# The value projection of both mixers multiplied unsplit in fp32, in a three-block network on one core

## The reference, cut to what matters

```python
for l in range(2):
    h = rms_norm(x, norm1_g[l]) * (1.0 + scale1) + shift1
    z = h @ w_in[l]                       # [256,1024] @ [1024,4608]
    q, k = z[..., 0:512], z[..., 512:1024]            # rotated, 4 heads x 2 x 64
    v    = z[..., 1024:1536]                          # 4 heads x 128
    o = diff_attention(q, k, v, lam)                  # two softmaxes, one minus lam times the other
    y_attn = rms_norm(o, subln_g[l]) * c @ w_attn_o[l]
    u = ga * sigmoid(gb); u = silu(layer_norm(conv31(u)))
    y_conv = u @ w_conv_o[l]
    x = x + (1 + gate1) * ((g_attn * y_attn + g_conv * y_conv) @ w_out[l])
    x = x + (1 + gate2) * ((silu(f_gate) * f_up) @ w_ffn_out[l])
```

## Time and profile before

| | us |
|---|---|
| median of 3 runs (2473.72 to 2474.51) | 2473.92 |
| the profiled execution, its own time | 2476.07 |
| span of the profile | 2474.3 |

### The profile page before, as it was taken

How to read it: one execution, slowest core, us unless ns; L and a number is a source line. 1 busy time by engine, 2 the same in 40 slices (tenths; PEclk the granted TensorE clock), 3 DMA queues, 4 the chain that set the end, 5 groups by cost and what they waited for, 6 DMA issues and landing times.

```text
span 2474.3 us, 29798 instructions
## 1 busy us (share of the span) xinstructions
PE 2368.3 (96%) x11879; PEld 1979.0 (80%) x11879; DVE 1938.3 (78%) x1864; ACT 1416.3 (57%) x1408; POOL 17.4 (1%) x33
## 2 busy tenths in 40 slices
PE   4988999998999899899999989999999999999998
PEld 4866788867888898798888978888888888888886
DVE  6997878787797656675445769898989898989897
ACT  2654433645543454455434547777777777777776
POOL 0000000000000000000000000000000000000000
PEclk9999999999999999899999989999999999999999
DMA  9556889434598445345555439999999999999996
GB/s 339 190 180 240 314 299 345 147 136 153 186 334 299 149 154 188 125 166 185 189 193 184 155 123 365 357 360 353 360 353 360 352 363 351 364 352 358 352 362 222
DMA packets 434768, 652.93 MB, mean 264 GB/s; under 512 B 20144, under 2 KB 323888, under 8 KB 434624
## 3 DMA queue, kind: packets, MB, share of 16 engines
q1 hardware_dynamic: 432592, 644.63, 75.9%
q0 software_dynamic: 2032, 6.33, 0.8%
HBM read 649.82 MB, written 1.05 MB: 263 GB/s over the span
## 4 chain that ended last, share of the span: by engine, by line
PE 90%; DVE 6%; ACT 2%; issue 1%; DMA 1%; SPq 0%; ACTq 0%; DVEq 0%
PE pair L2019 27%; PE pair L2021 27%; PE pair L2020 27%; PE pair L2054 3%; PE tb L2230 2%; PE pair L2411 1%; DVE aw L1516 1%; DVE rest L1147 1%; PE pair L2142 1%; DMA raw<-in_ada_w 1%; PE tb L2097 1%; DVE gat L1166 1%; ACT aw L722 0%; PE pair L2155 0%; DVE hT L1266 0%
## 5 line engine op out<-in xcount | busy, mean ns | idle before, releaser
L1147 DVE TENSOR_TENSOR rest<-raw,head 128x2048 fp32r<-128x2048 f32 x542 | 1240.6, 2291 | 300.6 <-ACT head L693 285.1
L693 ACT ACTIVATE head<-raw 128x2048 fp32r<-128x2048 f32 x542 | 1035.7, 1912 | 340.3 <-PE pair L2021 300.6
L2019 PE MATMUL pair<-head,hTh 128*128 128x512 f32 x1848 | 739.2, 400 | 4.7 <-DVE rest L1147 2.2
L2021 PE MATMUL pair<-head,hTl 128*128 128x512 f32 x1848 | 723.0, 391 | 0.0
L2020 PE MATMUL pair<-rest,hTh 128*128 128x512 f32 x1848 | 722.2, 391 | 0.0
L2019 PEld LDWEIGHTS pair<-head,hTh 128*128 128x128 f32 x1848 | 348.6, 189 | 77.3 <-issue 7.0
L2021 PEld LDWEIGHTS pair<-head,hTl 128*128 128x128 f32 x1848 | 348.0, 188 | 74.0
L2020 PEld LDWEIGHTS pair<-rest,hTh 128*128 128x128 f32 x1848 | 349.0, 189 | 69.2 <-issue 1.2
L2019 PE MATMUL pair<-head,aTh 128*128 128x512 f32 x776 | 308.6, 398 | 4.9 <-issue 3.8
L2021 PE MATMUL pair<-head,aTl 128*128 128x512 f32 x776 | 304.2, 392 | 0.0
L2020 PE MATMUL pair<-rest,aTh 128*128 128x512 f32 x776 | 304.0, 392 | 0.0
(11 more groups left out here) (302 smaller groups left out, 1653.2 us busy)
## 6 DMA issues: line engine op xcount, KB each, us to landing
raw<-in_moe_w_gate SPq DMA_DIRECT2D x224, 512.0 KB, 5.3
raw<-in_moe_w_up SPq DMA_DIRECT2D x224, 512.0 KB, 7.1
raw<-in_moe_w_down SPq DMA_DIRECT2D x224, 512.0 KB, 5.8
raw<-in_w_in SPq DMA_DIRECT2D x152, 512.0 KB, 4.6
raw<-in_ada_w SPq DMA_DIRECT2D x96, 512.0 KB, 5.7
raw<-in_w_ffn_in SPq DMA_DIRECT2D x88, 512.0 KB, 5.6
raw<-in_w_ffn_out SPq DMA_DIRECT2D x44, 512.0 KB, 5.4
raw<-in_w_out SPq DMA_DIRECT2D x40, 512.0 KB, 4.5
```

The lines of the kernel that those rows point to most:

```text
L693: act.activation(head[:, c.split, :], raw[:, c.raw, :], ACT.Copy).then_inc(heads_done, 1)
L1147: dve.tensor_tensor(rest[:, c.split, :], raw[:, c.raw, :], head[:, c.split, :].bitcast(F32), ALU.subtract).then_inc(rests_done, 1)
L2019: pe.matmul(out_, lh, rh, start=start, stop=False, skip_group_check=True)
L2021: return pe.matmul(out_, ll, rh, start=False, stop=stop, skip_group_check=True)
```

## The change

The plan's line for the job `v` of layers 0 and 1 gets `unsplit=True`. Nothing else in the file changes; the other differences follow from the set of unsplit chunks.

```diff
@@ -232,7 +232,7 @@
         plan_linear(f"q{l}", w, 512, "act", 0)
         plan_linear(f"k{l}", w, 512, "act", 512)
         plan_rotate(l)
-        plan_linear(f"v{l}", w, 512, "act", 1024)
+        plan_linear(f"v{l}", w, 512, "act", 1024, unsplit=True)
         plan_scores(l)
         plan_linear(f"gates{l}.0", w, NT, "act", 2560, unsplit=True)
         plan_linear(f"gates{l}.1", w, NT, "act", 2560 + NT, unsplit=True)
```

## The result

| | before | after |
|---|---|---|
| median, us (runs) | 2474.51 (2470.73 to 2475.55, 9) | 2479.61 (2478.70 to 2482.22, 9) |
| ratio, 95% interval | | 1.0027 (1.0019 to 1.0036) |
| span of the profile, us | 2474.3 | 2480.2 |
| time of the profiled execution, us | 2476.07 | 2482.22 |

The change costs 5.1 us by the medians; by the ratio it is 0.27%, 6.7 us, with an interval of 4.7 to 8.9 us. It is slower. The forecast was +5.8 and 2479.7 us, from a median of 2473.9 us of the kernel before; over all nine runs that median is 2474.5. The spans differ by 5.9 us.

A forecast was written before the change was run, and what follows sets the result against it. PE was taken to bound the kernel, with job v on the chain of waits in both mixers. 2 x 2.91 = +5.8 us on a median of 2473.9 gave 2479.7 us, range 2476.3 to 2483.0 us.

The forecast's parts named there:

- The term of PE: PE's job v, unsplit 13.84 us against 10.93 us split: +2.91 us for each mixer.
- Rival 3: At v, an unsplit product costs four short passes: +3.66 us a mixer, +7.3 in all, 2481.2 us; chance 0.03.
- DVE and ACT at nothing: DVE's lost rests (4.48 us a mixer) and ACT's lost heads (3.8 us) are hidden by waits and count nothing.
- Rival 4: DVE was the bound ahead of the head norm's reciprocal: 4.48 us a mixer come off, 2464.9 us; chance 0.04.
- SP's queue: Loads of gate 2's two chunks wait for PE's v, issued at 107.1 and 114.0 us; cost nothing.
- rival 5: Gate 2's chunks land late and PE waits: 2 us a mixer, 2483.7 us; chance 0.02.
- Downstream whole: Behind gates 0 and 1, the 2.91 us delay is handed on whole, unless the clock takes part.
- The prediction's own sign: Wrong if v under 12 us, chain on DVE before head norm, or feed-forwards not beginning +2.9 and +5.8 us later.
- rivals 1 and 2: Slow PE restarts after gaps shrink or vanish (+3.6 or +1.4 us, 0.20), or lengthen or appear (+7.2 to +8.6, 0.10).

The follow-up runs named there:

- the doubled one: The change with each unsplit matmul of v made twice, against the kernel before: 2507.24 against 2474.81 us, ratio 1.0140.
- the two halves: Change with v's heads and rests still made: 2479.05 us; split passes kept, v's heads and rests not made: 2473.45 us; both against the kernel before, 2473.87 us.
- the one-pass kernel: Kernel before with only the head by head pass of v, one of three, heads and rests still made: 2471.27 against 2474.81 us, ratio 0.9987.
- The single-mixer kernels: v unsplit in the first mixer only, or in the second only, against the kernel before: 2476.86 and 2476.77 against 2473.87 us, both 1.0012.

## Why the prediction was right

**The term of PE.** Predicted 13.84 - 10.93 = 2.91 us a mixer; measured 13.73 - 10.93 = 2.80. The price was taken from gates 0 and 1, half of a piece of 64 records; v's 32 records are 0.429 us apart on the mean, a little under the gates' 0.4325. This is the only term of the sum that was off, by 0.1 us a mixer. That the median itself was met to 0.1 us is luck: the step of 5.8 us was put on a median of three runs 0.6 us under that of nine, and the medians are 5.1 us apart. Rival 3, four short passes or 3.66 us, is out: 2.80 in both mixers, and 16.55 for the doubled one.

**DVE and ACT at nothing.** Shown by the two halves: with the rests kept the stretches are the same to 0.01 us, with the rests removed and PE's passes kept they are those of the kernel before to 0.02 us. DVE was to begin the rotation 1.3 us sooner in the first mixer; from the rotation's first matmul it was 3.03 us and is 2.01, 1.0 sooner. DVE's mask was to move by 1.8 us in the first mixer; measured from the rotation's start it moved from 18.08 to 19.86 us. The wait before the reciprocal was to become about 2 us; it is 1.79. Rival 4 is out; the one-pass kernel shows what its condition looks like in a trace, a reciprocal with no idle time before it.

**SP's queue.** Predicted issues at 107.1 and 114.0 us, measured 106.05 and 112.92, in an execution whose rotation began 1.0 us earlier. Nobody waits for these chunks; rival 5 is out.

**Downstream whole.** From the reciprocal to the turning of the channels it is 21.67 and 21.68 us before, and the same after, in both mixers. Further on the single spans move by 2 us either way. The single-mixer kernels at +3.0 and +2.9 us, and above all the doubled one, with 33.1 us in the stretches and 30.7 to 38.4 in the timing, agree with a delay that is handed on whole.

**The prediction's own sign.** It would count as wrong a first and a second feed-forward that begin by other than +2.9 and +5.8 us. In the chains, the activations for them (L1275, the last piece ahead of PE) come at 253.21 and 642.09 us before, at 256.97 and 647.19 after: +3.8 and +5.1 us. Taken to the letter the sign failed. The pieces are -1.0 us ahead of the first rotation, +2.81 in the first stretch with a v and +1.9 told below, which give +3.8; then +2.78 in the second stretch with a v, and -1.0 told below; the last half microsecond of the +5.1 stays open. The sign asked more of one pair of profiles than they can give.

**The clock, rivals 1 and 2.** In these two profiles both happened, in places, and on the whole they cancelled. In the first mixer two records and part of a third stood 0.43 us apart where 8 did in the earlier trace rows, which gave back 1.1 us (chain of waits after):

```profile
218.59 0.43 PE pair L2019
219.02 0.43 PE pair L2020
219.44 0.35 PE pair L2021
219.79 0.23 PE pair L2019
```

After the second mixer's channels are turned, 9 records (584.38 to 588.13 us) stood 0.43 us apart instead of 14:

```profile
584.38 0.77 PE L2019 MATMUL pair<-head,aTh 128*128 128x512 f32 x1 [1.00 <-issue]
...
587.50 0.63 PE L2020 MATMUL pair<-rest,aTh 128*128 128x512 f32 x1
587.93 0.53 PE L2021 MATMUL pair<-head,aTl 128*128 128x512 f32 x1
588.29 0.40 PE L2019 MATMUL pair<-head,aTh 128*128 128x512 f32 x1
```

which gave back 1 us against the earlier trace rows. At the end of the first mixer a new slow stretch stood where the clock had been full, and cost 1.6 us by the chain:

```profile
240.00:245.00 5.00, 3.93 (x29) 3.87 (x29) 1.70 (x7) 2.20 (x4) 0.00 (x0) 0.85 0.44 174
245.00:250.00 5.00, 5.00 (x21) 4.16 (x21) 3.25 (x9) 1.26 (x2) 0.00 (x0) 0.81 0.00 0
```

Ahead of both, on the chain of waits, a load of the output weights took 7.55 us instead of 6.67, and one of its issues on SP's queue 0.95 instead of 0.43. The first two lines are before and after, the other two the kernel with the first mixer only and the one with heads and rests kept:

```profile
200.02 6.67 DMA raw<-in_w_out
202.37 7.55 DMA raw<-in_w_out
201.74 6.60 DMA raw<-in_w_out
200.82 6.48 DMA raw<-in_w_out
```

These three give 1.4 - 1.1 + 1.6 = 1.9 of the +1.98 us of the third stretch in the table.

The last two of these kernels have v unsplit in the first mixer just as the change has. Their loads take about what it took before, and their granted clock is 1.00 from 235 to 275 us. So the late load and the new slow stretch belong to that execution and are not what the change does. The slow records behind the second mixer's channels vary as well: 14 before, 9 after, 7, 12 and 11 in the kernels with the first mixer, the second mixer and the splits kept. That the change alters them is not shown. The page "TensorE: Matmul & The Clock Gate" of the Trainium skill, section "What's actually happening", says that the throttled state is the default and activity releases it; the traces agree where the earlier trace rows has 0.50 at 210 to 215 us, behind a gap of PE, and 1.00 in the stretch of v, but not every gap is followed by a lower clock, as the 2.92 us in the one-pass kernel show.

**What stays open.** The ratio says +6.7 us (4.7 to 8.9), the medians +5.1, the chain +5.6. Nine runs of each kernel cannot tell 5.6 from 5.1 or from 6.7; that the change costs more than its 5.6 us on the path is not shown. The prediction took 4.9 us for what cannot be told from none; the intervals here reach about 2 us to either side, and 3.0 us in one mixer was told from none.

## What to carry to other kernels

Unsplit fp32 trades PE time (2.8 us for a product of 256 x 1024 by 1024 x 512) for the time of the engines that prepare the split (4.5 us of DVE, 3.8 of ACT). In this kernel it pays where one of these is last, as at gate 1, and costs where it is not, as at v, and the trace says so before any run: an engine with idle time in front of the next shared wait has nothing to gain from less work. Price the change by a stretch between two fixed points of the program, since such stretches repeat to 0.02 us while the timed executions of one kernel spread over 3 to 8 us. And where work is added to an engine with slack, look at what stands ahead of it in that engine's order, not only at the sum of its work.

## What the runs showed of the hardware

- An fp32 matmul of the program is two records in the trace, 0.4325 us each at 512 columns; the short form is one of 0.228 us. One product unsplit takes as long as 3.8 short ones, so the three short passes of the split take 21% less of PE than one unsplit product; over the whole job v it is 10.93 against 13.73 us.
- The same 2.20 us gap of PE, at the same place of two kernels that differ in DVE's and ACT's work, was followed by a granted clock of 0.67 in one execution (1.7 us lost on the scores) and of 1.00 in the other.
- Behind the turning of the second mixer's channels, 7 to 14 records stood 0.43 us apart in the profiles, each 0.2 us more than at the full clock. A change that moves work by a few microseconds is measured with this spread on it.
